# HGRN scores of a hybrid backbone step: six masked levels summed on GpSimd, placing, output product and update one unit later

## The reference

```python
b = jnp.cumsum(lf, axis=2)
dec = masked_exp(tri, b[:, :, :, None, :] - b[:, :, None, :, :])
A = jnp.einsum('bhik,bhjk,bhijk->bhij', qc, kc, dec)
o = jnp.einsum('bhik,bhkv->bhiv', qc * jnp.exp(b), S) + A @ vc
bl = b[:, :, -1]
S = S * jnp.exp(bl)[..., None] + jnp.einsum('bhck,bhcv->bhkv', kc * jnp.exp(bl[:, :, None] - b), vc)
```

## Time and profile before

| | us |
|---|---|
| median of 3 runs | 2394.53 |
| the runs | 2394.1 to 2400.58 |
| the profiled execution, its time | 2384.78 |
| its span | 2383.0 |
| mean granted TensorE clock | 0.952 of full |
| PE busy | 2139.2 (90%) |
| DVE busy | 1455.7 (61%) |
| ACT busy | 1282.7 (54%) |
| POOL busy | 754.4 (32%) |

### The profile page before, as it was taken

How to read it: one execution, slowest core, us unless ns; L and a number is a source line. 1 busy time by engine, 2 the same in 40 slices (tenths; PEclk the granted TensorE clock), 3 DMA queues, 4 the chain that set the end, 5 groups by cost and what they waited for, 6 DMA issues and landing times.

```text
span 2383.0 us, 54672 instructions
## 1 busy us (share of the span) xinstructions
PE 2139.2 (90%) x23118; PEld 1324.6 (56%) x23118; DVE 1455.7 (61%) x1807; ACT 1282.7 (54%) x1674; POOL 754.4 (32%) x557
## 2 busy tenths in 40 slices
PE   5998987978989999999899878888879999999994
PEld 4765656745565555555675558655544444444442
DVE  3156746668262221215558667585479999999985
ACT  3443754556443333423443665465268787878763
POOL 0422115433404242423233135432123333333332
PEclk8999998988999999999999889988979999999997
DMA  9322990020303131316221000110366777990114
GB/s 284 101 90 74 292 327 12 4 58 10 104 18 106 53 106 53 106 53 169 76 100 39 1 10 4 33 29 22 133 230 213 241 264 276 328 336 38 36 62 185
DMA packets 215385, 278.46 MB, mean 117 GB/s; under 512 B 28177, under 2 KB 188797, under 8 KB 215039
## 3 DMA queue, kind: packets, MB, share of 16 engines
q1 hardware_dynamic: 203776, 243.60, 31.7%
q0 software_dynamic: 8432, 29.89, 3.4%
q10 hardware_dynamic: 2959, 1.83, 0.3%
HBM read 368.35 MB, written 29.11 MB: 167 GB/s over the span
## 4 chain that ended last, share of the span: by engine, by line
PE 54%; issue 16%; DVE 13%; POOL 8%; ACT 5%; DMA 3%; SPq 1%; POOLq 0%; ACTq 0%; DVEq 0%
PE ps L2263 51%; POOL mix L969 5%; DVE arena L1653 2%; DMA wbuf<-in_w_mod 1%; DVE mix L1661 1%; DVE mix L1653 1%; DVE xT L1653 1%; PE ps L2470 1%; ACT arena L1143 1%; DVE mix L1657 1%; DVE hT L1653 1%; DVE arena L1657 1%; POOL mix L972 1%; SPq L701 1%; DVE mix L1790 1%
## 5 line engine op out<-in xcount | busy, mean ns | idle before, releaser
L2263 PE MATMUL ps<-hT,mix 128*128 128x512 f16 (+2 forms) x3024 | 381.1, 289 | 27.2 <-DVE hT L1653 14.4
L2263 PE MATMUL ps<-w,xgT 128*128 128x512 f16 x1632 | 365.3, 381 | 2.5 <-ACT xgT L1537 2.5
L2263 PEld LDWEIGHTS ps<-hT,mix 128*128 128x128 f16 x3024 | 231.1, 100 | 175.3 <-issue 23.2
L2163 DVE SCALAR_TENSOR_TENSOR w<-wst,w 128x2048 f16<-128x2048 f32 x136 | 309.9, 2319 | 22.8 <-ACT w L1524 22.8
L1001 POOL TENSOR_TENSOR a<-aval,a 128x256 f16<-128x256 f32 x68 | 159.0, 2338 | 371.2 <-ACT a L1572 371.2
L2263 PEld LDWEIGHTS ps<-w,xgT 128*128 128x128 f16 x1632 | 157.4, 98 | 181.1 <-issue 2.8
L1524 ACT ACTIVATE w<-wst 128x2048 f16<-128x2048 f32 x136 | 251.5, 1898 | 3.4 <-DMA xs_rows<-htok,slot_i 3.4
L2263 PE MATMUL ps<-mix 128*128 128x512 f16 (+5 forms) x1856 | 204.7, 288 | 14.5 <-POOL mix L972 8.8
L2263 PE MATMUL ps<-hT,arena 128*128 128x128 f16 (+1 forms) x1440 | 198.5, 299 | 1.0 <-DVE const L1653 1.0
L2263 PE MATMUL ps<-w2m,aT 128*128 128x512 f16 x816 | 188.8, 381 | 5.5 <-DVE aT L2201 5.5
L2263 PEld LDWEIGHTS ps<-mix 128*128 128x128 f16 (+3 forms) x1856 | 121.2, 124 | 89.3 <-POOL mix L972 12.4
(11 more groups left out here) (363 smaller groups left out, 3584.3 us busy)
## 6 DMA issues: line engine op xcount, KB each, us to landing
wst<-in_moe_w SPq DMA_DIRECT2D x204, 1024.0 KB
wbuf<-in_w_mod SPq DMA_DIRECT2D x40, 1024.0 KB
wbuf<-in_ffn_w SPq DMA_DIRECT2D x33, 1024.0 KB
wbuf<-in_w_in SPq DMA_DIRECT2D x20, 1024.0 KB
xs_rows<-in_table SPq DMA_DIRECT2D x17, 512.0 KB, 6.4
ys_rows<-yb POOLq DMA_DIRECT2D x17, 512.0 KB, 4.0
wbuf<-in_w_out SPq DMA_DIRECT2D x32, 256.0 KB
xg<-xs_rows POOLq DMA_DIRECT2D x16, 512.0 KB, 5.5
```

The lines of the kernel that those rows point to most:

```text
L2163: v_.scalar_tensor_tensor(out=q[1], in0=staged(s, p), scalar=WS, in1=q[0], op0=ALU.mult, op1=ALU.subtract).then_inc(sg["m_lo13"], 1)
L2263: return mm_(o, w, x, start=first, stop=last, skip_group_check=True)
```

## The change

Of the five sums of a chunk's levels, POOL makes those of chunks 0 to 3, after its `carried_q(4n + 4)` in unit x = 3, with the same three adds; DVE keeps the fifth, and waits ahead of it for POOL's count. ACT's `place` moves from x = 0 (ahead of `keys`) to x = 1 (ahead of `wide`), PE's `carry` from x = 1 to x = 2, DVE's `update` from x = 2 to x = 3 (ahead of `keys`), and ACT's start on the first output weight from u = 18 to u = 19. The plan of slot 1 follows.

```diff
-            j += [f"1:hs{n - 1}"] if x == 1 and n else []
+            j += [f"1:hs{n - 1}"] if x == 2 and n else []
@@ POOL
+                def collect(n):
+
+                    A = AC[n % 2]
+                    L.done(f"{l}.A{4 * n + 3}")
+                    L.do(g.tensor_tensor(A[:, 0:3], A[:, 0:3], A[:, 3:6], ALU.add))
+                    L.do(g.tensor_tensor(A[:, 0], A[:, 0], A[:, 1], ALU.add))
+                    L.made["ac_ready"] = 5 * l + n
+                    L.do(g.tensor_tensor(A[:, 0], A[:, 0], A[:, 2], ALU.add), "ac_ready")
+
+                    if x == 3 and n < 4:
+                        collect(n)
@@ ACT
-                    if x == 0 and n:
-                        place(n - 1)
                     if x == 0 and n < 4:
                         keys(n + 1)
+                    if x == 1 and n:
+                        place(n - 1)
                     wide(u)
-                    if u == 18:
+                    if u == 19:
                         L.full(J("hs3"))
                         upper(l, "wo0")
@@ DVE
                 def collect(n):
 
                     A = AC[n % 2]
+                    dve.wait_ge(sg["ac_ready"], 5 * l + 4)
+                    L.made["ac_ready"] = 5 * l + 4
-                    if x == 2 and n:
+                    if x == 3 and n:
                         update(SH, L.full(J(f"hs{n - 1}")), ebl[(n - 1) % 3], J(f"hs{n - 1}"), n - 1, 6)
-                    if x == 3:
+                    if u == UNITS - 1:
                         collect(n)
@@ PE
-                    if x == 1 and n:
+                    if x == 2 and n:
                         carry(n - 1)
```

## The result

The changed kernel is slower: 2411.09 us (median of 8 runs, 2406.38 to 2424.28) against 2395.24 for the kernel before on the same chip (8 runs), a ratio of 1.0069 [1.0051, 1.0088]. That is 12 to 21 us more, where 1.3 us less was predicted, and it lies outside the range of 2386 to 2402.

The account below looks back on a forecast made before the run. DVE was taken to bound most of the loop in both HGRN stages. Both layers gave -0.7 + 0.9 - 1.5 = -1.3 us on the profiled 2384.78; adding the 9.8 us difference to the runs gave 2393.2, range 2386 to 2402.

Parts of the forecast that it names:

- Part 1: Loop, four chunks a layer: sums moved to POOL take 1.9 us a chunk from DVE for 1.91 given back.
- The walk: POOL's adds from the chunk's last near mask: first add ends at 2.71 us, sum ready at 4.9, at most 5.8.
- The rival in which POOL has the turn each time: Loop: each collect blocks DVE for 3.07 us, not 1.9; +9.4, less 1.3, gives 2402.6; chance 0.12.
- The hidden block: Loop: POOL's adds cost DVE only 0.5 us a chunk and PE becomes the bound; -8.5 us, 2386; chance 0.15.
- the late placing: Loop: PE waits some 0.5 us a chunk for `AH`, as ACT's copy comes late; 2397; chance 0.15.
- Parts 2 and 3: Loop up to T, the end of `weigh(19)`: fewer DVE waits and collisions with POOL's 512-wide product; gains 3.0 and 2.5 us.
- the `update` wants carry 4.3 us after A: in time: Loop: `carry` takes 3.4 us at full clock, so DVE's `update`, 4.3 us after job A, needn't wait.
- Part 4: End of loop: waiting for near mask 19 loses 2.3 us of layer 0's 3.0; layer 1 is taken to gain 1.5.
- the 0.9 us set aside for a gap: Layer 0's loop end: half of A19's earlier 1.80 us gap, counted as loss in case it recurs on the path.

Follow-up runs that it names:

- shift_only: Changed kernel with all five sums back on DVE, while placing, product, update and the weight's start stay one unit later; ratio 1.0054 to the kernel before.
- update_late: Kernel before with only DVE's update of chunks 0 to 2 moved one unit later, to x = 3; ratio 1.0020 to the kernel before.
- after_again: The changed kernel run again without any edit, beside the kernel before on the same chip; ratio 1.0058.
- tail_only: Kernel before with chunk 3 alone late and the weight's start at u = 19, all sums on DVE; ratio 1.0056 to the kernel before.
- wo_18: Changed kernel with ACT's start on the first output weight back at u = 18; ratio 1.0043 to the kernel before.
- filler: Changed kernel with four more 128x512 matmuls on PE at u = 17, whose result nobody reads; ratio 1.0068 to the kernel before.
- weight_first: Kernel before with ACT's split of the first output weight put ahead of wide(18); ratio 0.9993 to the kernel before.
- last_old: Changed kernel with chunk 3 (its sum included) and the weight's start put back as before; ratio 1.0006 to the kernel before.

## Why the prediction was wrong

**Part 1 (the adds) was right in what it takes from DVE.** POOL's and DVE's timelines of the changed kernel at the end of chunk 0:

```profile
552.68 2.66 POOL L938 TENSOR_TENSOR mix<-mix 128x768 f32<-128x768 f32 x1 [0.43 <-DVE mix L1664]
555.42 1.46 POOL L939 TENSOR_TENSOR mix<-mix 128x256 f32<-128x256 f32 x1
556.96 1.63 POOL L941 TENSOR_TENSOR mix<-mix 128x256 f32<-128x256 f32 x1
```

```profile
551.98 0.56 DVE L1664 TENSOR_TENSOR mix<-ps,nearb 128x384 f32<-128x384 f32 x1
552.57 1.09 DVE L1664 TENSOR_TENSOR arena<-arena,mix 128x896 f32<-128x896 f32 x1
553.70 2.59 DVE L1664 TENSOR_TENSOR arena<-arena,extra 128x896 f32<-128x896 f32 x1
...
558.04 1.50 DVE L1664 TENSOR_TENSOR arena<-arena,extra 128x896 f32<-128x896 f32 x1
```

From the near mask's end (552.54) the first add ends at +2.80 (walked: 2.71), DVE's second product loses 1.50 (1.41), the one behind the mask 0.41 (0.4 to 0.5), and the sum is ready at +6.05. The walk had 4.9, and 5.8 at most: the third add came 0.05 us behind DVE's next product (556.91) and waited for that one as well. 1.9 us are taken from DVE for the 1.91 given back, and the timed runs agree: 1.0054 for shift_only, 1.0058 for the whole change. The averages agree (from 513 to 598 us; the earlier trace rows had 1097 for the first form):

```profile
L1664 DVE TENSOR_TENSOR arena<-arena,mix 128x896 f32<-128x896 f32 x27 | 32.2, 1193 | 0.9
L1664 DVE TENSOR_TENSOR arena<-arena,extra 128x896 f32<-128x896 f32 x11 | 18.2, 1655 | 0.4
```

The rival in which POOL has the turn each time (+9.4) therefore isn't what made it slower, though its sum of 2402.6 was the nearest. The rule of the Trainium skill ("SBUF — State Buffer", Who interferes with whom) held in its strict form but for 0.14 us: DVE's product lost 1.50 of the 1.64 us for which the add still ran. The hidden block falls with the same rows, and the late placing too: from 518 to 597 us the view of waits has PE waiting for ACT's exponentials (6.1 us in 4 times) and for nothing shown (9.4), never for the placing.

**Parts 2 and 3 (3.0 + 2.5 us gained before T) came only in part.** In the two profiles each, entry to T took 160.1 and 157.7 us before, both layers added, and 156.0 and 159.0 after: 1.5 us on the mean, less than the two profiles of one kernel differ. The step that failed is "the `update` wants carry 4.3 us after A: in time". Waits of 0.57 us for the product stand there even at full clock, so it missed by 0.6. At 566.59 DVE wanted it 3.0 us after job A, not 4.3, for the near mask ahead of it had itself waited 1.19 us for A:

```profile
DVE mix L1664 <- PE ps L2276: 2.0, 2, 1.2
DVE hT L1664 <- PE ps L2276: 0.6, 1, 0.6
```

These are DVE's waits of the changed kernel, 546 to 598 us. The 0.5 us for L1282 of the earlier trace rows is gone, and these have come in its place. update_late says the same from the other side: where PE is behind, the time that a DVE step gives up is waited away at the next mask.

**Part 4 (the end of the loop) was the step that broke the forecast.** "A18 ends at T - 1.3, the carry at T + 2.1, A19 at T + 3.6, the mask at T + 4.2." Measured in layer 0 (the 0.9 us set aside for a gap isn't in the first column):

| | predicted | changed kernel |
|---|---|---|
| A18 ends, `carry(3)` begins | T - 1.3 | T + 0.8 |
| the carry ends | T + 2.1 | T + 6.7 |
| near mask 19 ends | T + 4.2 | T + 8.9 |
| ACT begins the weight (0.9 behind the mask before it) | T + 5.1 | T + 9.7 |

Two terms were mis-sized. The larger is the carry's clock: I counted 3.4 us for layer 0 and named half clock only for layer 1, as one of two equal cases; it took 5.6 to 5.9 us in both layers of all five kernels in which chunk 3 is late and PE isn't filled (changed, after_again, shift_only, tail_only, wo_18). The other is a gap of 1.5 to 1.9 us in A18 of layer 0, ahead of the carry; I had placed it in A19 and counted half of it, 0.9, since before it stood there.

I had read the slow pieces of the earlier trace rows as bad luck of a stretch, and not asked what the change does to PE ahead of it. In the old order `carry(3)` fills PE between A17 and A18; in the new one PE waits there for `weigh(18)`, and in these ten cases it was busy 1.95 to 2.4 of the 4 us before its clock fell, which came between 0.4 us ahead of A18 and the first pieces of the carry. `carry(3)`, now on the path, then runs at half clock. In the two profiles of the kernel before the clock also fell at the end of layer 0's loop, but at 586.8 and 597.9, behind `carry(3)` and job A18; in layer 1 it fell ahead of `carry(3)`, for all of it in one profile and for part of it in the other. What was a slow stretch in which ACT and POOL set the pace became a slow stretch that everything waits for. filler shows that the clock hangs on this: with PE kept busy at u = 17 it stays at 1.00 in both layers.

The wait to the weight, 2.8 us in layer 0 and on the mean 4.5 in layer 1 before, became 9.7 to 10.0 and 8.3 to 8.4: about 7.1 + 3.8 = 10.9 us lost. The prediction had 2.3 + 0.9 = 3.2 for layer 0, and 1.0 for layer 1, since the 1.5 us that it gained there hold the 2.5 of the loop: 4.2 in all. So the wait costs 6.7 us more than forecast: 3.9 in layer 0 and 1.7 in layer 1 by the two terms, and 1.1 because the profile that the forecast was read from had a `carry(3)` at half clock in layer 1 itself (its wait there is 5.7, the second profile's 3.4). With the smaller gain in the loop, 4.0 (5.5 - 1.5), the sum is -1.3 + 6.7 + 4.0 = +9.4, and the two profiles' stages give 9.9. The timed difference is 15.9 us, 12.2 to 21.1 by the interval; what is missing can't be placed with profiles that scatter by 5 us. tail_only alone is 13.4 by the runs and 13.2 by the stage (330.0 against a mean of 316.8).

**Open.** What makes the gap in A18 isn't shown, but it doesn't hang on PE's idle time. It hangs on a count. Number PE's records in the trace (matmuls, weight loads and semaphore instructions) in order of start:

- In all five kernels with a late chunk 3 and no filler the gap of layer 0 stands ahead of record 16321, in A18. In the eight traces whose chunk 3 isn't late it stands ahead of record 16577, in A19, with 1.5 to 2.0 us.
- The 14 traces have 69 gaps of 0.8 us or more in the two loops in which PE runs nothing and waits for nothing shown. Within each layer all of them stand a multiple of 256 records apart. In filler the first gap of layer 1 stays at record 34905, as in all others, though 16 records more came before it.
- Which of the two places shows a gap goes with the time that PE took for the 256 records ahead of it: 2.9 to 4.0 us ahead of 16321 in the late kernels and 1.7 to 2.0 ahead of 16577 in the old order, but 4.7 us and more wherever there is no gap, 5.3 ahead of 16321 in filler among them.

A 16 KB packet of the "instruction" queue runs at 594.47 to 595.50, next to the gap that begins at 595.39, and before the gap of the earlier trace rows had one as well at 582.78 to 583.93. That PE waits there for the next block of its instructions fits all this, but no run tried it. In the stretch from 594 to 596.5 us of the changed kernel the DMA view has this packet alone:

```profile
q8 instruction: 1, 0.02, 2.6%
```

Open too is whether a filler no longer than the hole would give time back, where the rest of the timed difference lies, and whether weight_first is worth 1 or 2 us.

## What to carry to other kernels

Before a job is moved behind its neighbour near the end of a loop, walk the engine that runs it through the new order and look for the hole it leaves: here an idle PE ran the moved job at half clock, and as that job now stood on the path, the price was the whole difference, 2.5 us each time. When two in-order engines hand work to each other, look which one is behind: a step put off on the other engine only moved the wait to the next step (update_late). Undoing the last iteration alone, and changing it alone (last_old, 1.0006, and tail_only, 1.0056), told that nearly the whole loss was at the end of the loop.

## What the runs showed of the hardware

- The granted clock fell to 0.50 (1.2 GHz) ahead of or within `carry(3)` in both layers of all five kernels in which chunk 3 is late and PE is not filled; in the changed kernel PE had been busy 2.00 and 2.06 of the 4 us before the fall, with the filler 4.00, and the clock held. A product of the same shape takes 0.69 us at half clock instead of 0.44, and tail_only shows the fall within one job: 0.43, 0.62, 0.69.
- Gaps of 1.5 to 2.0 us in which PE waits for nothing shown fall in the dense streams of 64x32 and 64x64 matmuls (A18 or A19), in the unchanged kernel too; within a layer all such gaps of 0.8 us or more stand a multiple of 256 PE records apart.
- POOL and DVE take turns on two SBUF operands almost strictly: POOL's 256-wide add, for which a POOL operation of that width needs 0.67 us undisturbed, took 1.46 and 1.63 between DVE's products, and DVE's 1.09 us product 2.59.
